# One projection chunk of 456 columns in place of chunks of 72 and 384 columns

## The reference, cut to what matters

```python
h = rms_norm(x, norm_mix[l])
(sq, sk, sv, dq, dk, dv, iq, ik, iw, hq, hf, hi, hg,
 g_sb, g_dsa, g_hg) = jnp.split(h @ w_in_l, _split_points(), axis=-1)
y_sb  = stick_breaking_attention(sq, sk, sv) @ w_sb_l
score = sum over j of iw[j] * relu(q_i[j] . k_i)        # q_i from iq, k_i from ik, 64 keys are kept
y_dsa = dsa_attention(q, k, dv, q_i, k_i, iw) @ w_dsa_l
o     = hgrn2(hq, hf, hi, lb)
x = x + (sigmoid(g_sb)*y_sb + sigmoid(g_dsa)*y_dsa + sigmoid(g_hg)*y_hg) @ w_out_l
x = x + square(relu(rms_norm(x) @ w_up[l])) @ w_down[l]
```

## Time and profile before

| | |
|---|---|
| median of 3 runs | 1643.03 us (1642.92 to 1643.25) |
| span of the profiled execution | 1642.0 us |
| TensorE (PE) busy | 1491.5 us, 91% |
| VectorE (DVE) busy | 765.5 us, 47% |
| ScalarE (ACT) busy | 319.4 us, 19% |
| moved by DMA | 380.28 MB, mean 232 GB/s |

### The profile page before, as it was taken

How to read it: one execution, slowest core, us unless ns; L and a number is a source line. 1 busy time by engine, 2 the same in 40 slices (tenths; PEclk the granted TensorE clock), 3 DMA queues, 4 the chain that set the end, 5 groups by cost and what they waited for, 6 DMA issues and landing times.

```text
span 1642.0 us, 20158 instructions
## 1 busy us (share of the span) xinstructions
PE 1491.5 (91%) x8400; PEld 1001.7 (61%) x8400; DVE 765.5 (47%) x1467; ACT 319.4 (19%) x653; POOL 22.7 (1%) x41
## 2 busy tenths in 40 slices
PE   8999999999999999999999999999997667656667
PEld 5687899899545888898999446755542212212212
DVE  2657665766665656767757656534321000000001
ACT  2234422122001125430122002334400000000000
POOL 0000000000000000000000002100000000000000
PEclk9999999999999999999999999999998777789889
DMA  8547134445452643224444446655699999999997
GB/s 308 188 154 255 52 103 154 154 172 188 154 181 83 218 149 107 104 103 154 154 155 174 185 156 207 207 205 194 267 386 409 409 409 409 409 409 409 409 410 309
DMA packets 134668, 380.28 MB, mean 232 GB/s; under 512 B 6260, under 2 KB 16628, under 8 KB 134384
## 3 DMA queue, kind: packets, MB, share of 16 engines
q1 hardware_dynamic: 131696, 369.60, 60.0%
q0 software_dynamic: 2880, 9.36, 1.9%
HBM read 377.31 MB, written 5.73 MB: 233 GB/s over the span
## 4 chain that ended last, share of the span: by engine, by line
PE 74%; DMA 17%; SPq 5%; DVE 3%; issue 1%; ACT 0%; DVEq 0%; ACTq 0%
PE bank L1430 12%; PE bank L1476 12%; PE bank L1091 10%; DMA ring<-in_w 10%; PE bank L1098 8%; DMA region<-in_w 6%; PE bank L1256 5%; PE bank L1230 3%; PE bank L1625 3%; SPq L910 3%; PE bank L1206 2%; PE bank L1182 2%; PE bank L1373 2%; PE bank L1525 2%; SPq L907 2%; PE bank L1403 1%
## 5 line engine op out<-in xcount | busy, mean ns | idle before, releaser
L1091 PE MATMUL bank<-hT,ring 128*128 128x256 f32 x832 | 186.7, 381 | 0.0
L1091 PEld LDWEIGHTS bank<-hT,ring 128*128 128x128 f32 x832 | 155.5, 190 | 24.1 <-issue 3.4
L1476 PE MATMUL bank<-region 128*128 128x512 f32 x320 | 140.6, 592 | 0.0
L1625 PE MATMUL bank<-region 128*32 128x512 f32 x640 | 90.9, 698 | 47.1 <-DMA region<-in_w 47.1
L1476 PEld LDWEIGHTS bank<-region 128*128 128x128 f32 x320 | 60.5, 190 | 74.6 <-issue 74.6
L1430 PE MATMUL bank<-region 128*128 128x128 f32 x768 | 100.5, 275 | 0.0
L1430 PEld LDWEIGHTS bank<-region 128*128 128x128 f32 x768 | 93.0, 192 | 0.0
L1625 PEld LDWEIGHTS bank<-region 128*32 128x32 f32 x640 | 18.5, 118 | 113.8 <-DMA region<-in_w 75.9
L1098 PE MATMUL bank<-ring,region 128*128 128x512 f32 (+2 forms) x224 | 72.2, 480 | 2.7 <-ACT region L1734 1.4
L1098 PE MATMUL bank<-ring,hT 128*128 128x512 f32 x160 | 71.7, 596 | 0.0
L2771 DVE TENSOR_TENSOR region<-bank,region 128x512 f32<-128x512 f32 x8 | 5.5, 692 | 139.0 <-ACT region L1989 139.0
(11 more groups left out here) (461 smaller groups left out, 2434.1 us busy)
## 6 DMA issues: line engine op xcount, KB each, us to landing
region<-in_w SPq DMA_DIRECT2D x48, 2048.0 KB, 23.9
ring<-in_w SPq DMA_DIRECT2D x31, 2048.0 KB, 23.8
ring<-in_w_in SPq DMA_DIRECT2D x27, 2048.0 KB, 8.1
ring<-in_w_up SPq DMA_DIRECT2D x16, 2048.0 KB, 8.2
ring<-in_w_down SPq DMA_DIRECT2D x32, 1024.0 KB, 6.2
own_slot<-in_w SPq DMA_DIRECT2D x8, 2048.0 KB, 23.9
ring<-in_w_out SPq DMA_DIRECT2D x6, 2048.0 KB, 8.1
ring<-in_w_in SPq DMA_DIRECT2D x6, 1536.0 KB, 7.3
```

The costliest lines, as they stand in the source:

```text
L1091: t = mm(b[:, 0:T], w[:, k, :], act[:, k, :], start=(k == 0), stop=(k == KD - 1))
L1476: t = mm(b[:, :], left[:, t2, :], right[:, t2, :], start=(c4 == 0 and t2 == 0), stop=(c4 == 7 and t2 == 1))
L1625: t = mm(b[32 * e:32 * e + 32, :], xg[:, 2 * c + k, 32 * e:32 * e + 32], w[e][:, 512 * k:512 * k + 512], start=(c == 0 and k == 0), stop=( ...
```

## The change

The chunks ik (72 columns) and sv (384 columns) become one chunk "si" of 456 columns, at the place where ik stood. Columns 0 to 383 are the values, 384 to 447 the index keys, 448 to 455 the index weights. It is loaded by two transfers into one slot. ScalarE copies the keys, the weights and now the values from one bank and frees it after the last. The chunks of the layers are 36 and 35.

```diff
--- before.py
+++ after.py
@@ -75,7 +75,7 @@
 PT_GAIN = (0, 0, 1, 1, 2, 2, 2, 3, 3, 3, 4, 5)
 
 
-PROJ = (("d", 512, 2), ("iq", 512, 2), ("ik", 72, 2), ("kv", 512, 2), ("hi", 256, 2), ("hg", 256, 2), ("sv", 384, 2),
+PROJ = (("d", 512, 2), ("iq", 512, 2), ("si", 456, 2), ("kv", 512, 2), ("hi", 256, 2), ("hg", 256, 2),
         ("hf", 512, 4), ("hq", 512, 4), ("sk", 384, 3), ("sq", 384, 3))
 
 
@@ -91,7 +91,7 @@
 def chunks_of_layer(l):
 
 
-    c = [(n, "w_mem_kv_2", 0, 0, w) if n == "kv" else (n, "w_in", 0, COL["dq" if n == "d" else n], w)
+    c = [(n, "w_mem_kv_2", 0, 0, w) if n == "kv" else (n, "w_in", 0, COL[{"d": "dq", "si": "sv"}.get(n, n)], w)
          for n, w, _ in projections(l)]
     c += [(("g", j), "w_in", 0, COL["gsb"] + 512 * j, 512) for j in range(6)]
     c += [(("br", j), "w_br", 0, 512 * j, 512) for j in range(2)]
@@ -538,7 +538,7 @@
         chunk_at = {c[0]: n for n, c in enumerate(chunks)}
         arrive, slot_total = [], [0] * MSLOTS
         for n, c in enumerate(chunks):
-            slot_total[n % SLOTS] += 16 * {"w_br": 3, "w_down": 2}.get(c[2], 1)
+            slot_total[n % SLOTS] += 16 * (2 if c[0][1] == "si" else {"w_br": 3, "w_down": 2}.get(c[2], 1))
             arrive.append((slot_full[n % SLOTS], slot_total[n % SLOTS]))
 
         exp_arrive = []
@@ -951,7 +951,7 @@
             sp.dma_start(slot(0)[:, 0:4, :], first[:, 0:4, :]).then_inc(first_half_loaded, 16)
             sp.dma_start(x[:, :, 512:1024], rows[:, :, 512:1024]).then_inc(x_late_loaded, 16)
             sp.dma_start(slot(0)[:, 4:8, :], first[:, 4:8, :]).then_inc(arrive[0][0], 16)
-            for n, (_, l, name, r0, kt, c0, w) in enumerate(chunks):
+            for n, (key, l, name, r0, kt, c0, w) in enumerate(chunks):
                 if n == 0:
                     continue
                 if n == 2:
@@ -972,6 +972,10 @@
                         rows = slice(D_FF // 2 * h + r0, D_FF // 2 * h + r0 + 2 * P)
                         sp.dma_start(s[:, 4 * h:4 * h + 4, :].rearrange("p (t n) f -> p t (n f)", t=2),
                                      a[name][l, rows, :].rearrange("(t p) n -> p t n", p=P)).then_inc(arrive[n][0], 16)
+                elif key[1] == "si":
+                    cols = a[name][l].rearrange("(k p) n -> p k n", p=P)
+                    sp.dma_start(s[:, 0:kt, 0:384], cols[:, :, c0:c0 + 384]).then_inc(arrive[n][0], 16)
+                    sp.dma_start(s[:, 0:kt, 384:w], cols[:, :, COL["ik"]:COL["ik"] + 72]).then_inc(arrive[n][0], 16)
                 else:
                     src = a[name][l, r0:r0 + kt * P, c0:c0 + w].rearrange("(k p) n -> p k n", p=P)
                     sp.dma_start(s[:, 0:kt, 0:w], src).then_inc(arrive[n][0], 16)
@@ -1262,7 +1266,7 @@
                 if l == 0:
                     turn_half(0, 0)
                 first_rows(N_MIX[l], [(l, "d", i) for i in range(NT)], arrived((l, "d")) if l else slot(0), raw_tile)
-                for name, cols, _ in projections(l)[1:7 if l == 0 else 6]:
+                for name, cols, _ in projections(l)[1:-4]:
                     if name == "hi":
 
                         pe.wait_ge(consts_loaded, 32)
@@ -1336,7 +1340,7 @@
                     elif kind == "o":
                         c = s[1]
                         if c == 0:
-                            wait_freed([(l, "sv", 0), (l, "sv", 1)])
+                            wait_freed([(l, "si", 0), (l, "si", 1)])
                         pe.wait_ge(sba_ready, l * 3 + c + 1)
                         b = bank_of(key)
                         heads = [(b[HD * hh:HD * hh + HD, :], HD * (2 * c + hh), sbL[:, 2 * c + hh, :]) for hh in range(2)]
@@ -1809,10 +1813,11 @@
                     t = A_(R[:, i, 8:16, :].rearrange("p (f h) d -> p f (h d)", f=2), four[:, :, i, :], ACT.Copy, scale=r_[i])
                 t.then_inc(rows_copied, 1)
                 for i in range(NT):
-                    b = read((l, "ik", i))
-                    A_(R[:, i, 16, :], b[:, 0:HD], ACT.Copy, scale=r_[i])
-                    A_(R[:, i, 17, :], b[:, 0:HD], ACT.Copy, scale=r_[i])
-                    free(A_(iw[:, i, :], b[:, HD:HD + N_IDX], ACT.Copy, scale=rs_idx[:, l, i:i + 1]), (l, "ik", i))
+                    b = read((l, "si", i))
+                    A_(R[:, i, 16, :], b[:, 384:384 + HD], ACT.Copy, scale=r_[i])
+                    A_(R[:, i, 17, :], b[:, 384:384 + HD], ACT.Copy, scale=r_[i])
+                    A_(iw[:, i, :], b[:, 384 + HD:456], ACT.Copy, scale=rs_idx[:, l, i:i + 1])
+                    free(A_(sv[:, i, :], b[:, 0:384], ACT.Copy, scale=r_[i]), (l, "si", i))
                 if l == 0:
                     norm(N_MEM)
                     act.wait_ge(rs_ready, N_MEM + 1)
@@ -1827,8 +1832,6 @@
                 t.then_inc(rows_copied, 1)
                 for i in range(NT):
                     A_(hsg[i], four[:, 1, i, :], ACT.Sigmoid, scale=r_[i]).then_inc(sig_ready, 1)
-                for i in range(NT):
-                    free(A_(sv[:, i, :], read((l, "sv", i))[:, 0:384], ACT.Copy, scale=r_[i]), (l, "sv", i))
                 if l == 0:
                     act.wait_ge(lb_shifted, 1)
                     A_(lb_e, lb_e, ACT.Exp).then_inc(lb_exps, 1)
@@ -2404,7 +2407,7 @@
                 if l == 0:
                     norm(N_MEM)
                 dve.wait_ge(rows_copied, 2 * l + 1)
-                for n in ("d", "ik"):
+                for n in ("d", "si"):
                     for i in range(NT):
                         dve.wait_ge(*bk.freed((l, n, i)))
                 q7 = R[:, :, 0:7, :]
```

## The result

The changed kernel takes 1684.41 us (median of 4 runs, 1683.94 to 1684.64) against 1643.14 us for the kernel before in the same session: a ratio of 1.0247, 95% interval 1.0234 to 1.026 (the quotient of the two medians is 1.0251). It is slower by 41.3 us.

What follows compares the result with a forecast made beforehand. TensorE was taken to bound the layers, the stream of expert weights the end; layer 0 3.3, layer 1 9.2, clock 5.8 and stream 23.1 sum to 41.4 us on 1643.0, giving 1684.4 us, range 1671 to 1692.

Steps and rivals of the forecast that it cites:

- layer 0, m5 later: Layer 0, TensorE: product m5 of hf waits for VectorE's last row sum and starts 3.3 us later.
- layer 1, m5 later: Layer 1, TensorE: product m5 of hf waits for VectorE's last row sum and starts 9.2 us later.
- start of the stream: Expert weight loads: chunk 12 gets its turn 23.1 us later, and the kernel's end moves by as much.
- The matmuls: Projections on TensorE: the merged 456-column group takes 12.25 us for 13.85, saving 1.60 us a layer.
- Place of the work, layer 1: Layer 1: VectorE's chain starts behind the merged group, so TensorE waits and the layer loses 9.2 us.
- Layer 0: Layer 0: the chain starts from kv's end, 8.72 us later; 5.5 us of slack leave a 3.3 us loss.
- The clock: TensorE behind the new idle times: granted clock falls once in each layer, 2.9 us a fall, 5.8 us.
- The experts' first chunks: Expert ring: with 81 chunks, unchanged EXP_SLOT makes chunk 3 wait for wo0, chunk 4 for wo1; +23.1 us.
- 1 (clock not falling): Both layers and stream lose as forecast, but the clock stays full: 1678.6 us; chance 0.30.
- 2 (stream doesn't matter): Experts' stream doesn't feel its late start, something else held chunk 12: 1661.3 us, or 1655.5 without falls; chance 0.07.
- 3 (chain isn't late): VectorE's chain isn't late in the layers, only the experts' stream is: 1662.9 us; chance 0.08.
- 4 (the saving carries through): TensorE ends 1.6 us earlier in each layer and this carries through to the end: 1639.8 us; chance 0.03.

Runs made afterwards that it cites:

- e7: e6 with three row sums of hT moved between the corner sums of hh, each with its own signal; 1640.36 us, 0.9977 of the kernel before.
- e8: The kernel before, nothing merged, with the two relaxations of VectorE's order from e6 and e7; 1643.32 us, ratio 1.0.
- e3: The kernel before with the values' projection moved directly behind the index keys', still two chunks; 1663.36 us, 1.0113 of before.
- e1: The changed kernel with the expert slots asked for in an order that fits its ring of 81 chunks; 1660.02 us, 1.0095 of before.
- e9: The same kernel as e1, run again on one chip in the same rounds as e10; 1660.12 us.
- e2: The kernel before with e1's slot order, the wrong one for its 83 chunks; 1666.86 us, 1.0139 of before.
- e6: e1 with VectorE's wait for the merged bank moved to where the keys are needed, in front of the rotation; 1643.86 us, 1.0001 of before.
- e10: e9 with filling matmuls, their results unread, in the idle times of both layers, same chip and rounds; 1656.49 us.
- e4: The changed kernel with matmuls whose result nobody reads, in layer 1 three of them behind the wait for hT; 1684.54 us, 1.0242 of before.

## Why the prediction was right, step by step

The forecast was 1684.4 us in 1671 to 1692, slower with 0.95. The total agrees to a tenth of a microsecond, which is luck: the two clock terms are 0.8 us too large together, and the profiled execution is 40.5 us longer where the medians are 41.3 apart and the forecast was 41.4. Measured on the two profiled executions:

| term | forecast | measured | read from |
|---|---|---|---|
| 456 columns, one group | 12.25 | 12.24 | 37.62 to 49.86 |
| layer 0, m5 later | 3.3 | 3.46 | 82.59 to 86.05 |
| layer 0, clock | 2.9 | 2.49 | m5 to end of hf: 13.21, was 10.72 |
| layer 1, m5 later | 9.2 | 9.18 | 539.49 to 568.96 was 29.47, now 38.65 |
| layer 1, clock | 2.9 | 2.54 | m5 to end of hf: 13.36, was 10.82 |
| start of the stream | 23.1 | 22.8 | a remainder: 40.5 between the spans less the 17.7 above |

- *The matmuls.* The rate per column of the wide group held. The saving of 1.6 us a layer is real, though the changed kernel doesn't show it: e7 does, 1.6 us in layer 0 and 1.65 in layer 1, 3.0 us against e8 by the medians.
- *Place of the work, layer 1.* Each figure of the step is in a row: VectorE starts 9.2 us later within its layer, hT's wait is 2.73 us (2.8 forecast), the last wait 7.75 ("some 8"). e3 shows the cause with nothing merged.
- *Layer 0.* The 5.5 us of slack were eaten as forecast, idle 4.71 us for 4.9. The step is short on how: VectorE's squares don't wait for kv (they start at 55.65, kv's projection runs from 53.05 to 66.86); what does is ScalarE's square root, which stands behind its copies of kv, and VectorE sits idle 5.38 us for it before the head norms.
- *The clock.* The mechanism was right in both layers and its size too large: 2.9 us taken from a place beside the experts, 2.5 here. It isn't a constant either: 1.3 to 2.8 us a fall in the three profiles of e1, e9 and the changed kernel. The rule of the Trainium skill ("TensorE: Matmul & The Clock Gate", section "HAM oscillation — how this bites in real kernels"), that waits throttle the array again, agrees with the 0.50 behind the 7.75 us of idle time here.
- *The experts' first chunks.* Chunk 3 with wo0's end, chunk 4 with wo1's, a hole of 40 us in the DMA traffic before. The eight chunks at the full rate don't show in the queue's rows, since SP issues chunks ahead of those still crossing: chunk 12 goes out at 1221.65, long before the 1219.4 + 17.7 at which the prediction gave it its turn. They show in the time left: 486.4 us from chunk 4 (1196.07) to the end, against 445.7 from chunk 12 (1196.28) before, 40.7 us more for a forecast of 41.0. e1 takes the term away (24.4 us by the medians, 25.3 against the kernel before of each occasion), e2 makes it alone (22.8). e1's figures hold what the price of the clock's fall differs by between executions as well, so e2's is the better one.
- *Rivals.* 1 (clock not falling) fell with the windows at 0.50; 2 (stream doesn't matter) with e1 and e2; 3 (chain isn't late) with the 7.75 us; 4 (the saving carries through) fell for the change as it was made, but its mechanism is what e7 has: it needs the chain early and the slots matched, close to the two conditions that the rival named.

What stays open: why the same idle time lets the clock fall sooner in one execution than in another, and so costs 1.3 us or 2.8; and where e6, whose chunk at wo0's end goes out 0.95 us before that of the kernel before, loses this lead until chunk 12 (1196.33 and 1196.28).

## What to carry to other kernels

When two pieces of work are merged, one of them moves, and it takes with it the cover it gave and the wait that others have on its partner; before counting the instructions saved, look for who is idle until the partner is done, and move that wait to the first real use. And where a ring is indexed by a running number, a chunk more or less rotates everything behind it: a hand-written order that was tuned to one rotation can be 20 us wrong at the other end of the kernel, in lines that the change doesn't touch.

## What the runs showed of the hardware

The same idle time can have either outcome for the clock. 2.73 us in front of the first products of hf left it at full in the changed kernel and in e1 (the 16 instructions behind took 2.02 us) and let it fall in e9 and e3 (3.45 and 3.55 us). Idle times of 1.39 and 1.80 us (e6) left it at full; 4.71 and 7.75 us let it fall.

Two executions of one kernel are therefore some us apart before anything is changed. e1 and e9 are the same kernel; their profiled spans are 3.2 us apart, and 2.2 of these stand already at the chunk that waits for wo0 (1186.34 and 1184.12), most of it the different price of the fall in layer 0. The last matmuls behind the last load ran at either level too: eight instructions took 3.70 us in the changed kernel, e1, e9 and e10, 4.44 in e7 and 4.86 in e4. A difference of 1 to 3 us between two medians has to be looked for in the trace, stretch by stretch between marks, before it is called the effect of an edit.
